# Sixteen of the gathered V rows are summed by TensorE instead of VectorE, and the gate round moves twelve rows

## The reference

```python
scores = einsum('bshpd,hpnd->bshpn', (h @ w_q), sub_keys)   # 8 heads, 2 x 128 keys
top_s, top_i = top_k(scores, 16)                            # per side
best_s, best = top_k(all 16 x 16 sums, 16)                  # 16 experts per token and head
gates = softmax(best_s)
act = gelu(einsum('td,ted->te', h, u_tab[idx]))             # 128 experts per token
out = einsum('te,ted->td', gates * act, v_tab[idx])
x = layer_norm(2 ** 0.25 * h + out)
```

## Time and profile before

| | |
|---|---|
| time, 3 runs | 1471.32 us median (1469.31 to 1473.35) |
| profiled execution | 1466.45 us, its span 1464.4 us |
| TensorE busy | 1339.9 us (92%) |
| VectorE busy | 1156.5 us (79%) |
| GpSimd busy | 664.8 us (45%) |
| ScalarE busy | 394.1 us (27%) |
| moved by DMA | 444.26 MB, of which gathers 268.47 MB; mean 303 GB/s |
| granted TensorE clock, mean | 0.964 |

### The profile page before, as it was taken

The page is one execution under the profiler, slowest core; times in us unless marked ns, Lnnn a source line. Parts: engine busy times, 40 slices in busy tenths (PEclk is TensorE's granted clock), DMA queues, the critical chain, the costliest instruction groups (busy, mean ns, idle before and its releaser), DMA issues.

```text
span 1464.4 us, 18719 instructions
## 1 busy us (share of the span) xinstructions
PE 1339.9 (92%) x6450; PEld 946.0 (65%) x6450; DVE 1156.5 (79%) x2505; ACT 394.1 (27%) x804; POOL 664.8 (45%) x548
## 2 busy tenths in 40 slices
PE   8999989799999999989999599999999999999900
PEld 6787755488888888867544255578888844444400
DVE  5836356778888898689889998878999887665788
ACT  5233001412120101169310155556541010000010
POOL 2244111444233245620335565645445575666672
PEclk9999999899999999999999799999999999999965
DMA  6411324686888889981699999999899999999995
GB/s 238 150 59 58 135 96 144 192 268 222 296 301 299 293 316 414 413 319 59 218 391 393 393 393 412 400 359 393 334 357 365 415 413 413 414 413 413 412 353 208
DMA packets 118429, 444.26 MB, mean 303 GB/s; under 512 B 11712, under 2 KB 24512, under 8 KB 101952
## 3 DMA queue, kind: packets, MB, share of 16 engines
q0 software_dynamic: 73728, 268.47, 48.2%
q1 hardware_dynamic: 44032, 173.56, 30.9%
q10 hardware_dynamic: 576, 1.05, 0.2%
HBM read 440.94 MB, written 2.10 MB: 303 GB/s over the span
## 4 chain that ended last, share of the span: by engine, by line
DVE 33%; PE 29%; DMA 15%; POOL 7%; issue 6%; DVEq 5%; ACT 4%; ACTq 1%; SPq 0%
DMA big<-in_peer_v_dram,idx 11%; DVE y L1178 8%; PE ps L1414 7%; DVE big L1157 7%; PE ps L1360 7%; PE ps L1343 6%; POOL big L609 4%; DMA big<-in_peer_u_dram,idx 3%; POOL big L599 3%; PE ps L1507 2%; PE ps L1598 2%; DVE work L1040 2%; ACT wr L659 1%; DVE topi L1039 1%; DVE top L1042 1%
## 5 line engine op out<-in xcount | busy, mean ns | idle before, releaser
L599 POOL DMA_INDIRECT big<-in_peer_u_dram,idx x256 | 309.4, 1209 | 536.5 <-DVE dots L1157 428.1
L1157 DVE CUSTOM_DVE_ANT_0 big<-big,xh 128x1024 f32<-128x1024 f32 x256 | 311.6, 1223 | 62.5 <-DMA big<-in_peer_u_dram,idx 40.1
L1178 DVE SCALAR_TENSOR_TENSOR y<-big,wgt,y 128x1024 f32<-128x1024 f32 x256 | 328.1, 1282 | 40.1 <-DMA big<-in_peer_v_dram,idx 35.5
L609 POOL DMA_INDIRECT big<-in_peer_v_dram,idx x256 | 294.4, 1150 | 106.0 <-issue 67.7
L1414 PE MATMUL ps<-big,pool_mem 128*128 128x512 f32 x512 | 224.3, 593 | 0.0
L1343 PE MATMUL ps<-xT,big 128*128 128x256 f32 x960 | 211.1, 380 | 0.0
L1343 PEld LDWEIGHTS ps<-xT,big 128*128 128x128 f32 x960 | 181.7, 190 | 24.3
L1414 PEld LDWEIGHTS ps<-big,pool_mem 128*128 128x128 f32 x512 | 96.7, 190 | 118.6 <-issue 118.6
L1414 PE MATMUL ps<-y,pool_mem 128*128 128x512 f32 x256 | 114.9, 599 | 0.0
L1414 PE MATMUL ps<-xT,pool_mem 128*128 128x512 f32 x256 | 113.5, 593 | 0.0
L1343 PE MATMUL ps<-xT,y 128*128 128x256 f32 x480 | 106.4, 380 | 0.0
(11 more groups left out here) (249 smaller groups left out, 1544.0 us busy)
## 6 DMA issues: line engine op xcount, KB each, us to landing
big<-u_pairs_dram SPq DMA_DIRECT2D x32, 1024.0 KB, 8.0
big<-v_pairs_dram SPq DMA_DIRECT2D x32, 1024.0 KB, 8.0
y<-u_pairs_dram SPq DMA_DIRECT2D x16, 1024.0 KB, 7.7
xT<-u_pairs_dram SPq DMA_DIRECT2D x16, 1024.0 KB, 7.7
y<-v_pairs_dram SPq DMA_DIRECT2D x16, 1024.0 KB, 7.9
xT<-v_pairs_dram SPq DMA_DIRECT2D x16, 1024.0 KB, 8.1
big<-in_w_in_dram SPq DMA_DIRECT2D x24, 512.0 KB, 5.6
pool_mem<-in_peer_w_q_dram SPq DMA_DIRECT2D x12, 1024.0 KB, 7.5
```

Of the source, the lines that this page charges most:

```text
L599: nc.gpsimd.indirect_dma_start(urow[n % RING], None, peer_u2, bass.IndirectOffsetOnAxis(ap=idx[:, u, e:e + 1], axis=0)).then_inc(s_u[n % R ...
L609: nc.gpsimd.indirect_dma_start(vrow[n % RING], None, peer_v2, bass.IndirectOffsetOnAxis(ap=idx[:, u, e:e + 1], axis=0)).then_inc(s_v[n % R ...
L1157: V.tensor_tensor_reduce(out=urow[n % RING], in0=urow[n % RING], in1=xh[:, u // PH * D:(u // PH + 1) * D], scale=1.0, scalar=0.0, op0=ALU. ...
L1178: V.scalar_tensor_tensor(acc_rows[t], vrow[n % RING], wgt[:, u % 2, e:e + 1], acc_rows[t], ALU.mult, ALU.add).then_inc(s_vadd, 1)
```

## The change

V rows 0 to 15 (unit 0) are no longer added by VectorE. For each, ScalarE writes a diagonal matrix of the weights (the identity, each row times its token's weight, job `diag`), and TensorE multiplies it with the V row in two products of 512 columns (job `vrow`), summing all sixteen in the two PSUM banks 0 and 1. The jobs stand behind the four query blocks of the last two heads (one row each) and behind the first six `act` jobs (two rows each). VectorE adds the sum to the accumulator of tile 0 once, at row 62, before the `selT` job puts other data into the same banks. `gather_v` of rows 6 to 21 waits for TensorE's use instead of VectorE's. The gate round stands at row 96 instead of 84; jobs `gelu` and `gates`, the later choices (units 7 to 11, now at 97, 103, 109, 114, 120; unit 12 stays at 174) and the loads of the last norm's gains move to suit. The scratch for GpSimd's descriptors is 4096 instead of 8192 bytes per partition, which makes room for four diagonals.

```diff
-ROUND_ROW = 84
+ROUND_ROW = 96
+PE_ROWS = 16
+QUERY_ROWS = 12
+PAIR_ROWS = 2
+PE_ROWS_ADDED = 62
-LATER_CHOICES = {ROUND_ROW + 1: 7, ROUND_ROW + 6: 8, ROUND_ROW + 12: 9, ROUND_ROW + 18: 10, ROUND_ROW + 24: 11, ROUND_ROW + 90: 12}
+LATER_CHOICES = {97: 7, 103: 8, 109: 9, 114: 10, 120: 11, 174: 12}
...
+    def with_rows(rows_, kind, *arg):
+        mine = [m for m in rows_ if 0 <= m < PE_ROWS]
+        for m in mine:
+            jobs.append(("diag", (m,), None))
+        add(kind, *arg, by="act")
+        for m in mine:
+            jobs.append(("vrow", (m,), None))
...
-        add("query", n, 0, by="act")
+        with_rows(range(2 * n - QUERY_ROWS, 2 * n - QUERY_ROWS + 1), "query", n, 0)
...
-    during = {(0, 2): 1, (0, 12): 2, (0, 26): 3, (1, 4): 8, (1, 11): 9, (1, 20): 10}
+    during = {(0, 1): 1, (0, 9): 2, (0, 19): 3, (1, 3): 9, (1, 9): 10, (1, 17): 11, (1, 26): 12}
...
+            if r == 0:
+                m = 2 * PH - QUERY_ROWS + PAIR_ROWS * n
+                with_rows(range(m, m + PAIR_ROWS), "act", 0, n)
+            else:
+                add("act", r, n, by="dve")
...
-            if (r, n) == (0, 21):
+            if (r, n) == (0, 17):
                 jobs.append(("gates", (), None))
...
+            if r == 0 and n == QUARTER:
+                for u in range(6, 7):
+                    jobs.append(("gelu", (u,), None))
-    between = {1: 6, 9: 7}
+    between = {2: 7, 10: 8}
-    dense_second_half(1, range(11, GUNITS))
+    dense_second_half(1, range(13, GUNITS))
...
-            for p in range(HALF + EARLY):
+            for p in range(HALF // 2 + EARLY + 8):
                 load_pair(p)
             sp.wait_ge(s_best, PH)
...
-                if n >= RING:
-                    pool.wait_ge(s_vadd, n - RING + 1)
+                if RING <= n < PE_ROWS + RING:
+                    pool.wait_ge(s_pv, n - RING + 1)
+                elif n >= RING:
+                    pool.wait_ge(s_vadd, n - RING + 1 - PE_ROWS)
...
+                if kind == "diag":
+                    m = arg[0]
+                    u, i = divmod(m, TOPK)
+                    act.wait_ge(s_wgt, u + 1)
+                    if m >= 4:
+                        act.wait_ge(s_pv, m - 3)
+                    A.activation(diag[:, m % 4, :], ident[:], ACT.Copy, scale=wgt[:, u % 2, i:i + 1]
+                                 ).then_inc(s_diag, 1)
+                    continue
...
+            def add_psum_rows():
+                dve.wait_ge(s_pv, PE_ROWS)
+                V.tensor_tensor(acc_rows[0], acc[0], acc_rows[0], ALU.add)
+                fence().then_inc(s_pvd, 1)
...
-                if n >= LAG:
+                if LAG <= n < LAG + PE_ROWS and n % TOPK == 0:
+                    weights((n - LAG) // TOPK)
+                    fence().then_inc(s_wgt, 1)
+                if n >= LAG + PE_ROWS:
                     add_row(n - LAG)
+                if n == PE_ROWS_ADDED:
+                    add_psum_rows()
...
+                if kind == "vrow":
+                    m = arg[0]
+                    if m == 0:
+                        for k in range(2):
+                            pe.wait_ge(free[k], USED[k])
+                    pe.wait_ge(s_diag, m + 1)
+                    pe.wait_ge(s_v[m % RING], 16 * (1 + m // RING))
+                    for half in range(2):
+                        last = T.matmul(ps[:, half, :], diag[:, m % 4, :],
+                                        vrow[m % RING][:, half * 512:(half + 1) * 512], start=(m == 0),
+                                        stop=(m == PE_ROWS - 1))
+                    last.then_inc(s_pv, 1)
+                    continue
...
-                        pe.wait_ge(s_alpha, 1)
+                        pe.wait_ge(s_pvd, 1)
...
-    nc = _bacc.Bacc("TRN2", target_bir_lowering=False, num_devices=1, dynamic_dma_scratch_size=8192)
+    nc = _bacc.Bacc("TRN2", target_bir_lowering=False, num_devices=1, dynamic_dma_scratch_size=4096)
```

More of the change, by code:

```diff
@@ L181, in static_jobs @@
             jobs.append(("gelu", (0,), None))
-        add("query", n, 0, by="act")
+        with_rows(range(2 * n - QUERY_ROWS, 2 * n - QUERY_ROWS + 1), "query", n, 0)
         if n:
             add("keys", n - 1, 0, by="act")
-        add("query", n, 1, by="act")
+        with_rows(range(2 * n - QUERY_ROWS + 1, 2 * n - QUERY_ROWS + 2), "query", n, 1)
         if n:
@@ L198, in dense_first_half @@
                     jobs.append(("onehot", (1, n + 1), None))
-            add("act", r, n, by="act" if r == 0 else "dve")
+            if r == 0:
[3 more added lines that the diff above has]
+                add("act", r, n, by="dve")
             if (r, n) in during:
                 jobs.append(("gelu", (during[r, n],), None))
-            if (r, n) == (0, 21):
+            if (r, n) == (0, 17):
                 jobs.append(("gates", (), None))
@@ L243, in static_jobs @@
     for i, (kind, arg, by) in enumerate(jobs):
-        if kind in ("split", "norm", "scale", "gelu", "gates", "expert", "onehot", "half", "early", "dnorm"):
+        if kind in ("split", "norm", "scale", "gelu", "gates", "expert", "onehot", "half", "early", "dnorm", "diag",
+                    "vrow"):
             placed.append((kind, arg, by, None, None))
@@ L383, in layer @@
         zsq = [pool_mem[:, 4096 + a * D:4096 + (a + 1) * D] for a in range(2)]
+        diag = sb("diag", [P, 4, P])
         iota = sb("iota", [P, NK])
@@ L451, in layer @@
         s_dot, s_gel, s_vadd = sem("dots_done"), sem("gelu_ready"), sem("vrows_added")
+        s_wgt, s_diag = sem("row_weights_ready"), sem("weight_diagonal_ready")
+        s_pv, s_pvd = sem("vrow_in_psum"), sem("psum_rows_added")
         s_blk = [sem(f"blocks_loaded{s}") for s in range(DPAIRS)]
@@ L554, in _ @@
             sp.dma_start(lnp2[:, 1, :], ln2_b[0].partition_broadcast(P)).then_inc(s_ln, 16)
-            for p in range(HALF + EARLY, 2 * HALF):
+            for p in range(HALF // 2 + EARLY + 8, 2 * HALF):
                 load_pair(p)
@@ L1161, in weights @@
             def weights(u):
+                if 2 <= u < PE_ROWS // TOPK + 2:
+                    dve.wait_ge(s_diag, TOPK * (u - 1))
                 dve.wait_ge(s_exp, u + 1)
@@ L1172, in add_row @@
                 t = u // PH
-                if n == 0:
+                if n == PE_ROWS:
                     dve.wait_ge(s_y, GATHERED)
@@ L1385, in _ @@
             for kind, arg, by, b, n in JOBS:
-                if kind in ("split", "norm", "scale", "gelu", "gates", "onehot", "half", "dnorm"):
+                if kind in ("split", "norm", "scale", "gelu", "gates", "onehot", "half", "dnorm", "diag"):
+                    continue
[11 more added lines that the diff above has]
+                    last.then_inc(s_pv, 1)
                     continue
```

## The result

| | before | changed |
|---|---|---|
| median of 4 runs | 1472.34 us (1469.31 to 1474.99) | 1491.19 us (1489.41 to 1495.18) |
| profiled execution, its span | 1466.45, 1464.4 us | 1495.18, 1493.4 us |
| TensorE busy | 1339.9 us | 1373.4 us |
| VectorE busy | 1156.5 us | 1139.0 us |

A forecast was written before the change was run, and what follows sets the result against it. Transfers bound VectorE's turns before the gate round, and TensorE's end sets the tail: 21.8 + 2.8 + 11.5 = 36.1 us later, less 25.8 us of slack, is 10.3 us over 1471.3, say 1482 us, range 1460 to 1489.

The forecast's parts named there:

- the round's start: Gate round moved to row 96: VectorE, held by transfers, arrives at 655.0 us, so the round starts 21.8 us later.
- GELU of unit 4: First addition behind the round: VectorE waits 2.8 us for ScalarE's GELU, delaying the first team and TensorE by 2.8 us.
- waits at two teams: Second set of teams: choices of units 12 and 13 make TensorE wait 2.9 and 8.6 us, together +11.5 us.
- rest of TensorE's run: TensorE behind the round: half clock costs 1 to 2 us at each new wait, left in the range.
- slack of the tail: Behind TensorE's end: the tail can shrink from 70.6 to 44.8 us, a gain of 25.8 us.
- The price: V rows on TensorE: sixteen products take 6.96 us, so the thirty-two added take 13.9 us.
- wait for rows that are then done: Other places of GELUs, gates and loads of the last norm's gains: they wait for rows already done; nothing added.
- The bytes: 22 turns from row 74: 23.1 MB of rows plus ten block pairs, 10.5 MB, at 413 GB/s take 81.3 us.
- The scratch: GpSimd's descriptors: half the scratch holds back no gathers, taken as nothing, with 5 us as upper bound.
- Rival (a): Turns before the round: transfers don't hold them, the round shifts 9.4 us; 1469, or 1459 to 1462 us; chance 0.22.
- rival (b): Second set of teams: the choices stay covered, TensorE doesn't wait there; 1470 us; chance 0.20.
- rival (c): More waits than counted, from half clock, held U rows and descriptors: 5 to 10 us more, 1487 to 1492; chance 0.10.

The follow-up runs named there:

- a_again: The changed kernel again, unchanged, as the reference for later runs: 1492.24 us, 1.0148 times the kernel before.
- experiment 1: The changed kernel with the second 512 columns of V rows 1 to 15 left out, 17 products on TensorE instead of 32: 1489.29 us, 1.0140.
- kernel 6: The changed kernel with the GELU of unit 4 early and the choices of units 12 and 13 at rows 186 and 190: 1472.81 us, 1.0014.
- experiment 2: The changed kernel with the GELU of unit 4 behind the 29th act job instead of behind the round: 1489.12 us, 1.0131.
- experiment 3: The changed kernel with the choices of units 12 and 13 moved to rows 186 and 190: 1477.69 us, 1.0053.
- experiment 9: Third chip: kernel before with scratch 4096 (0.9992), unit 11's choice late (0.9968), units 10 and 11 late (0.9975); changed kernel with four choices late, GELU early (1.0239).
- experiment 7: The changed kernel with only one of two blocks loaded for block pairs 18 to 31 of the first half: 1486.79 us, 1.0106.
- the last kernel on that chip: The changed kernel with the GELU of unit 4 early and the choices of units 10 to 13 late, on the third chip: 1535.37 us, 1.0239.

## Why the prediction was wrong

The mechanism was right in its outline: transfers hold the turns ahead of the round, the round starts when VectorE arrives, TensorE then runs to its end with every new wait added, and TensorE sets the tail. The sizes, term by term, from the profile on record and from the second one (a_again), each with its head taken off:

| term | predicted | changed | a_again |
|---|---|---|---|
| the round's start | +21.8 | +31.7 | +28.2 |
| GELU of unit 4 | +2.8 | +2.9 | +2.9 |
| waits at two teams | +11.5 | +12.4 | +12.5 |
| rest of TensorE's run | 0, left in the range | +3.3 | +3.0 |
| TensorE's end | +36.1 | +50.3 | +46.6 |
| slack of the tail | -25.8 | -25.3 | -25.4 |

**The step that failed** is the arrival at the round, +21.8 us, which measured +28.2 to +31.7. Two counts inside it were too small: the price of the work handed to TensorE, and the bytes of the block pairs that come in front of the round.

*The price.* "Sixteen products of this shape take 6.96 us, so 13.9 us". The "x16" of the earlier trace rows counts instructions, of which a float32 product has two. The text had the means to see it: a pair of V blocks is 2 x 4 products, and the prediction itself gives it 6.94 us. The 32 products took 27.6 us. A V row thus costs TensorE 1.73 us, while VectorE gains 1.24 us by it (rows 32 to 48 take 19.9 us less, head taken off).

TensorE's own lateness was absorbed by its wait for the round, of which 11.0 us (7.75 in a_again) are left where 15 were predicted. The price worked through VectorE. Experiment 1 is the test, for its 17 products take some 14.6 us, near the 13.9 that were predicted. Stretch by stretch, heads taken off:

| | predicted | experiment 1 | a_again | changed |
|---|---|---|---|---|
| VectorE's gain, rows 32 to 48 | 22.7 us | 21.6 | 20.2 | 19.9 |
| its loss, rows 48 to 74 | 1.4 us | 0.6 | 3.3 | 4.6 |
| the 22 turns from row 74 | 81.3 us | 84.6 | 83.6 | 85.2 |
| block pairs moved in these turns | 10.5 MB | 11.54 | 11.81 | 12.58 |
| the round's start | +21.8 us | +25.3 | +28.2 | +31.7 |

With 15 products less VectorE is at row 74 at 573.9 us, against the 573.7 of the prediction's count; a_again has 577.8 and the profile on record 579.7. So the doubled price made VectorE 3.8 to 5.8 us late by row 74. The traces show three ways in which this can come about. GpSimd loads V rows later: its waits for TensorE's use of them (L1444) come to 66.8 us in the changed kernel and 53.4 in experiment 1. In the profile on record VectorE waits for rows from row 62 on. In a_again it waits at row 66 for the `gates` job of ScalarE, which stands behind a block of TensorE that is late; the prediction had put this job among what "wait for rows that are then done". Timeline of VectorE in a_again:

```profile
561.07 0.42 DVE L1179 TENSOR_REDUCE dsum<-gated 128x16 f32<-128x256 f32 x1 [2.10 <-ACT gated L715]
```

Experiment 1 has no such wait. What each of the three costs by itself was not tried.

*The bytes.* Even with the price nearly as predicted the round starts 3.5 us too late, 3.3 of them in the 22 turns. The DMA queue of the block pairs in them (packets, MB, share), experiment 1 and the changed kernel:

```profile
q1 hardware_dynamic: 1584, 11.54, 32.9%
```

```profile
q1 hardware_dynamic: 1728, 12.58, 35.7%
```

The rate held: 34.92 and 35.20 MB in all, at 413 GB/s, are 84.6 and 85.2 us. The count of ten pairs did not. Experiment 1 issues ten in that stretch, and one issued before it (at 574.04 us) lands in it (583.40). TensorE ends its first half 14 us before VectorE arrives, so all eleven land in front of the round, the last at 655.5 us. In the kernel before, one pair is under way at row 74 (590.88 to 598.79 us) and one at the round (629.64 to 638.00), so five issued are 5.05 MB moved: the check that gave 38.1 against 38.2 us came out because the two ends cancelled, and that was luck. The changed kernel issues eleven, since TensorE's first half lasts 13 us longer than in experiment 1, and the one under way makes twelve.

**The rest of TensorE's run**, 3.0 to 3.3 us, was put down to half clock behind the waits and left out of the sum. With the two team waits gone and the first team as before (kernel 6) it is 1.3 us: TensorE ran 1426.3 - 866.5 = 559.8 us from the first team, against 558.5. So some 2 us come with the two waits; the granted clock is 0.83 over 1085 to 1095 us and 0.70 over 1111 to 1120 in the changed kernel.

**What held.** GELU of unit 4: waits of 1.24 and 1.36 us at the place foretold, and experiment 2 takes them away. The waits at teams 10 and 12: 4.4 and 8.0 us, predicted 2.9 and 8.6, and experiment 3 takes them away and gives 13 us. The tail, 45.2 us for 44.8; but VectorE came to row 272 at 1441.7 us and not at 1420. Its wait there, 11.85 us for some 15, is near the forecast only because TensorE was late too. The scratch, nothing (experiment 9). Rival (a) falls by experiment 7, rival (b) by the team waits, and rival (c), a few more microseconds on the same mechanism, to which I gave one chance in ten, holds the median with its 1487 to 1492 us. That is partly luck: half clock and the order of the V rows are there, but the bytes of the pairs and the doubled price, the larger part, are not in it, and the descriptors cost nothing. The chance for its kind was too low, since every bound left out of the sum lay on that one side.

Where the 20 us of VectorE went is thus settled. The engine came earlier to the turns ahead of the round and waited there for transfers (34.5 us against 13.3); the twelve turns put in front of the round to use the lead had to be paid at some 3.8 us each in place of 2.56, since the same 1.05 MB had to come with each while the pairs went on.

## What to carry to other kernels

Price an operation by the instructions that the trace counts, not by the calls in the source, and check the price on a stage whose products you can count; then compare what a row costs the engine that takes it with what it frees (here 1.73 against 1.24 us). Before moving a meeting point of two engines, ask what bounds the turns that are put in front of it: where the transfers are full, VectorE's lead buys nothing. Count the bytes of a stretch with what is under way at both its ends. And what stands at fixed row numbers has to move with the point (13 us here), while the wait that is already there is the place for a gain: taking two choices out of the stretch before the first team gave the kernel before 0.41%.

## What the runs showed of the hardware

On the chip of experiment 9 TensorE got single instructions in a stretch where the other chips gave it an unbroken run (busy in all 10 us from 600 to 610 us in the earlier trace rows). The kernel before with the small scratch shows it in its timeline of TensorE:

```profile
602.06 0.38 PE L1343 MATMUL ps<-xT,big 128*128 128x256 f32 x1 [1.07 <-issue]
604.90 0.59 PE L1343 MATMUL ps<-xT,big 128*128 128x256 f32 x1 [2.46 <-issue]
607.02 0.59 PE L1343 MATMUL ps<-xT,big 128*128 128x256 f32 x1 [1.54 <-issue]
```

The two next kernels of experiment 9, with unit 11 and with units 10 and 11 late, show it there too (TensorE's first half ends at 662.8 to 664.0 us in all three, and at 630.5 in the same kernel on the fourth chip), and the second of them once more from 834 to 851 us, so that its first team starts 15.8 us after VectorE was ready; their ratios are those of a disturbed kernel. In the last kernel on that chip this lasted a whole stage. Its windows, as above:

```profile
580.00:600.00 20.00, 17.93 (x82) 15.24 (x81) 18.94 (x25) 4.01 (x7) 15.39 (x16) 0.99 0.99 391
600.00:660.00 60.00, 17.59 (x30) 8.62 (x30) 48.66 (x62) 0.60 (x1) 43.09 (x42) 0.50 1.03 410
```

30 instructions in 60 us, each some 2 us behind the last, with no wait for a semaphore in the profile, the clock granted at half, and the DMA engines full with gathers. Its DMA queues in 600 to 660 us:

```profile
q0 software_dynamic: 6458, 23.51, 98.3%
...
q8 instruction: 1, 0.02, 0.1%
q14 instruction: 2, 0.02, 0.1%
```

TensorE's first half ended at 732.2 us instead of some 660: 72 us, of the same kind as the 66.5 between the two medians of this kernel (1535.37 and 1468.87). That the instructions themselves came late behind the gathers would fit, but it is only argued: three packets in the instruction queues say little, the more so as the undisturbed changed kernel on the fourth chip has four in the same 60 us. Each chip was measured on one occasion, so chip and occasion can't be told apart, and why this one does it and the three others do not stays open. For reading ratios it means that a kernel can owe some per cent to them (1.0239 there, 0.9993 on the fourth).
